# First-block borders by half rows, gain as a row, and turns with one PSUM bank per half of the tokens

## The reference, cut to what matters

```
first block, per layer l:
    h = h + 0.5 * rms_norm(swiglu(rms_norm(h, ffn1_pre_g)), ffn1_post_g)
    u = rms_norm(h, mix_pre_g);  four mixers on u @ w_in, merged by gates
    h = h + rms_norm(merged @ w_o, mix_post_g)
    h = h + 0.5 * rms_norm(swiglu(rms_norm(h, ffn2_pre_g)), ffn2_post_g)
second block, per layer i:
    x = layernorm(ALPHA*x + 0.5*swiglu_2(x), ln_g[i,0], ln_b[i,0])
    x = layernorm(ALPHA*x + hybrid_mixer(x), ln_g[i,1], ln_b[i,1])
    x = layernorm(ALPHA*x + 0.5*swiglu_2(x), ln_g[i,2], ln_b[i,2])
rms_norm(x, g) = x * rsqrt(mean(x*x) + 1e-6) * g
```

## Time and profile before

| | |
|---|---|
| Time before, median of 3 runs | 3259.92 us (3257.59 to 3264.05) |
| Profiled execution, its own time | 3261.25 us |
| Its span, first to last instruction | 3259.6 us |
| TensorE busy | 3045.4 us, 93% of the span |
| VectorE busy | 1881.4 us, 58% |
| ScalarE busy | 1340.2 us, 41% |
| GpSimd busy | 524.2 us, 16% |
| Mean granted TensorE clock | 0.966 |

### The profile page before, as it was taken

How to read it: one execution, slowest core, us unless ns; L and a number is a source line. 1 busy time by engine, 2 the same in 40 slices (tenths; PEclk the granted TensorE clock), 3 DMA queues, 4 the chain that set the end, 5 groups by cost and what they waited for, 6 DMA issues and landing times.

```text
span 3259.6 us, 59469 instructions
## 1 busy us (share of the span) xinstructions
PE 3045.4 (93%) x22178; PEld 2883.8 (88%) x22178; DVE 1881.4 (58%) x3364; ACT 1340.2 (41%) x2214; POOL 524.2 (16%) x791
## 2 busy tenths in 40 slices
PE   8999999999999999998898988999989998899998
PEld 7989998998989999897798878989989897899897
DVE  4556876555555876555455467455555546653555
ACT  4344454434334454433334544434333355443332
POOL 0000000000000000000003555440000055456000
PEclk9999999999999999999998999999999999999999
DMA  5544445454554445455663222254546522123453
GB/s 205 186 161 150 140 146 182 165 185 159 185 180 148 140 146 171 166 190 156 191 215 128 95 78 79 79 181 162 202 146 222 178 96 99 66 79 135 164 196 130
DMA packets 72445, 495.51 MB, mean 152 GB/s; under 512 B 8064, under 2 KB 8240, under 8 KB 20176
## 3 DMA queue, kind: packets, MB, share of 16 engines
q1 hardware_dynamic: 67824, 471.95, 42.2%
q0 software_dynamic: 4048, 18.59, 2.1%
q10 hardware_dynamic: 272, 0.99, 0.1%
HBM read 487.31 MB, written 4.19 MB: 151 GB/s over the span
## 4 chain that ended last, share of the span: by engine, by line
issue 71%; PE 16%; POOL 5%; DVE 4%; DVEq 1%; ACT 1%; POOLq 1%; DMA 1%; ACTq 0%; SPq 0%
PE psum L1153 5%; POOL weights_low L942 4%; PE psum L1065 4%; PE psum L1122 1%; PE psum L1263 1%; POOL small L898 1%; DMA weight_ring<-stream 1%; PE psum L1490 1%; DVE work L2260 1%; POOLq L897 1%; PE psum L1367 1%; PE psum L1209 1%; PE psum L1488 0%; PE psum L1478 0%; ACT weights_high L1558 0%
## 5 line engine op out<-in xcount | busy, mean ns | idle before, releaser
L1558 ACT ACTIVATE weights_high<-weight_ring 128x2048 fp32r<-128x2048 f32 (+5 forms) x778 | 906.0, 1184 | 1121.1 <-DMA weight_ring<-stream 1113.9
L1881 DVE TENSOR_TENSOR weights_low<-weight_ring,weights_high 128x2048 fp32r<-128x2048 f32 (+4 forms) x538 | 888.1, 1658 | 789.7 <-ACT weights_high L1558 786.8
L1065 PE MATMUL psum<-normed_t_high,weights_high 128*128 128x256 f32 x2816 | 801.4, 285 | 11.3 <-DVE normed_t_low L1890 9.9
L1065 PE MATMUL psum<-normed_t_low,weights_high 128*128 128x256 f32 x2816 | 798.9, 284 | 0.0
L1065 PE MATMUL psum<-normed_t_high,weights_low 128*128 128x256 f32 x2816 | 798.6, 284 | 0.0
L1065 PEld LDWEIGHTS psum<-normed_t_high,weights_high 128*128 128x128 f32 x2816 | 541.7, 192 | 17.7 <-DVE normed_t_low L1890 12.3
L1065 PEld LDWEIGHTS psum<-normed_t_low,weights_high 128*128 128x128 f32 x2816 | 542.4, 193 | 3.2
L1065 PEld LDWEIGHTS psum<-normed_t_high,weights_low 128*128 128x128 f32 x2816 | 542.1, 193 | 0.0
L1122 PE MATMUL psum<-weights_high,work_parts 128*128 128x512 f32 x1472 | 464.1, 397 | 13.5 <-DVE work_parts L1890 13.5
L942 POOL TENSOR_TENSOR weights_low<-weight_ring,weights_high 128x256 fp32r<-128x256 f32 x560 | 410.6, 765 | 223.3 <-ACT weights_high L1558 223.3
L1153 PE MATMUL psum<-normed_t_high,weights_high 128*128 128x256 f32 x1248 | 392.1, 314 | 2.8 <-DVE normed_t_low L1890 2.1
(11 more groups left out here) (267 smaller groups left out, 4347.0 us busy)
## 6 DMA issues: line engine op xcount, KB each, us to landing
weight_ring<-stream SPq DMA_DIRECT2D x400, 1024.0 KB, 4.9
weight_ring<-stream SPq DMA_DIRECT2D x64, 768.0 KB, 4.2
feature_rows<-feat POOLq DMA_DIRECT2D x6, 1024.0 KB, 7.6
work<-toeplitz_rows POOLq DMA_DIRECT2D x8, 512.0 KB, 6.5
feature_rows<-feat POOLq DMA_DIRECT2D x6, 512.0 KB, 4.1
toeplitz_rows<-work POOLq DMA_DIRECT2D x1, 3072.0 KB, 36.6
params<-prms POOLq DMA_DIRECT2D x5, 251.5 KB, 3.6
residual<-x SPq DMA_DIRECT2D x2, 512.0 KB, 4.8
```

The source lines that it names most:

```text
L1065: ins = pe.matmul(PS[:, bank, at:at + S], w[a][:, first + k, c * P:(c + 1) * P], src[b][:, k, :], start=(k, m) == (0, 0), stop=(k, m) == ( ...
L1558: return act.activation(dst, src, ACT.Copy, scale=scale)
L1881: dve.tensor_tensor(some(LOW, i, q, n), some(RING, i, q, n), some(HIGH, i, q, n).bitcast(F32), ALU.subtract).then_inc(low_by_vector, n)
```

## The change

- **post**: ScalarE sums the squares of each half row as soon as its bank is full (four Squares of 128x512 into a buffer of its own, `SQ`). GpSimd adds the two sums (`rsqrt_of_halves`: add, drain, add, drain, power). VectorE multiplies each bank by the gain row already behind the Square, without the root (`gained`), and then adds root x product to `H` in one instruction per half row, with a drain behind each (`added`).
- **norm**: ScalarE squares each half row. VectorE scales `H` by the root and by the gain row of the norm, `PG[:, 1]`, into `XN`, four instructions of 128x512, in place of the two scaled identities. Both gain rows come with one transfer of 1024 KB. The first one of the kernel has a transfer of its own at the start.
- **xt in both blocks**: a bank now holds one half of the tokens and four feature blocks (jobs in the order t = 0 half 0, t = 0 half 1, t = 1 half 0, t = 1 half 1). TensorE turns `XN` by transposes in both blocks. In the first block ScalarE copies a bank in one 128x512 and VectorE subtracts in one 128x512. In the second block ScalarE needs four 128x128 per bank for gain and bias. The first product waits for the banks of both t before k = 0 and again before k = 4.
- **post2**: `scaled` runs in two instructions of 128x512, each with its own signal.

The diff, cut to its core (left out: the plans' signal counts, credits, the parameter table without its three gains, and the layout on the host):

```diff
+def rsqrt_of_halves(dst, halves, eps, signal, count):
+    for n in range(2):
+        pool.wait_ge(squares_summed, reach("squares_summed", count + n))
+        pool.tensor_tensor(dst, dst if n else EPSES[:, EPS_AT[eps], 0:1], halves[:, n:n + 1], ALU.add)
+        pool.drain()
+    pool.tensor_tensor(dst, dst, HALFNEG[:, 0:1], ALU.pow).then_inc(signal, 1)
...
-    pool.wait_ge(residual_ready, reach("residual_ready", 2 * st.s if now.blk == 1 else 4 * (st.s + 1)))
+    pool.wait_ge(residual_ready, reach("residual_ready", 4 * st.s if now.blk == 1 else 4 * (st.s + 1)))
     if now.blk == 2 and st.s == 1:
         pool.wait_ge(delta_out_ready, reach("delta_out_ready", NH_B))
     if now.blk == 1:
-        row = feat1[bass.ds(now.l, 1), st.s:st.s + 1, :].rearrange("a b n -> (a b) n")
-        pool.dma_start(PG[:, 0, :], row.to_broadcast([P, D])).then_inc(feature_rows_loaded, 16)
-    else:
-        row = feat2[bass.ds(now.l, 1), st.s].rearrange("a c n -> a (c n)")
-        pool.dma_start(PG[:].rearrange("p c n -> p (c n)"), row.to_broadcast([P, 2 * D])
-                       ).then_inc(feature_rows_loaded, 16)
+        normed = named(("norm", st.s)).at["normed_ready"]
+        pool.wait_ge(normed_ready, reach("normed_ready", normed))
+    row = (feat1 if now.blk == 1 else feat2)[bass.ds(now.l, 1), st.s].rearrange("a c n -> a (c n)")
+    pool.dma_start(PG[:].rearrange("p c n -> p (c n)"), row.to_broadcast([P, 2 * D])
+                   ).then_inc(feature_rows_loaded, 16)
...
+pool.dma_start(PG[:, 1, :], feat1[0, 3, 1:2, :].to_broadcast([P, D])).then_inc(feature_rows_loaded, 16)
...
-        if fresh is not None and k % 2 == 0:
-            ready = named(("xt", fresh)).jobs[k // 2]
-            pe.wait_ge(bank_taken[ready.bank], taken_at(ready))
+        if fresh is not None and k % 4 == 0:
+            for t in range(T):
+                ready = named(("xt", fresh)).jobs[2 * t + k // 4]
+                pe.wait_ge(bank_taken[ready.bank], taken_at(ready))
...
-    n = named(("norm", st.s)).at["normed_ready"] if now.blk == 1 else 2 * st.s
-    for t in range(T):
-        pe.wait_ge(normed_ready, reach("normed_ready", n - 1 + t))
-        for k in range(KB):
-            job = st.jobs[k // 2]
-            if t == 0 and k % 2 == 0:
-                pe.wait_ge(bank_taken[job.bank], turn_at(job))
-            dst = PS[:, job.bank, (k % 2 * T + t) * P:(k % 2 * T + t + 1) * P]
-            if now.blk == 1:
-                ins = pe.matmul(dst, H[:, t, k * P:(k + 1) * P], DG[:, t, :], start=True, stop=True, skip_group_check=True)
-            else:
-                ins = pe.transpose(dst, XN[:, t, k * P:(k + 1) * P], IDENT)
-            if t == T - 1 and k % 2:
-                ins.then_inc(bank_full[job.bank], 1)
+    first = (named(("norm", st.s)).at["normed_ready"] if now.blk == 1 else 4 * st.s) - 3
+    for n, job in enumerate(st.jobs):
+        t, half = n // 2, n % 2
+        pe.wait_ge(bank_taken[job.bank], turn_at(job))
+        pe.wait_ge(normed_ready, reach("normed_ready", first + n))
+        for kk in range(4):
+            k = 4 * half + kk
+            ins = pe.transpose(PS[:, job.bank, kk * P:(kk + 1) * P], XN[:, t, k * P:(k + 1) * P], IDENT)
+        ins.then_inc(bank_full[job.bank], 1)
...
 def norm(st):
-    for t in range(T):
-        act.wait_ge(residual_ready, reach("residual_ready", 2 * st.s - 1 + t))
-        act.activation(XN[:, t, :], H[:, t, :], ACT.Square, scale=D ** -0.5,
-                       accum_out=SS[:, t:t + 1]).then_inc(squares_summed, 1)
+    for n in range(2 * T):
+        t, cols = n // 2, slice(n % 2 * HALF, (n % 2 + 1) * HALF)
+        act.wait_ge(residual_ready, reach("residual_ready", 4 * st.s - 3 + n))
+        act.activation(XN[:, t, cols], H[:, t, cols], ACT.Square, scale=D ** -0.5,
+                       accum_out=SSN[:, n:n + 1]).then_inc(squares_summed, 1)
...
-    for k2, job in enumerate(st.jobs):
+    for n, job in enumerate(st.jobs):
+        t, half = n // 2, n % 2
         act.wait_ge(bank_full[job.bank], full_at(job))
-        b = job.bank
+        src = PS[:, job.bank, :].rearrange("p (k n) -> p k n", k=4)
         if now.blk == 1:
-            g = prm(f"g{st.s}", 1)
-            for kk in range(2):
-                k = 2 * k2 + kk
-                last = copy(XTH[:, k, :], PS[:, b, kk * S:(kk + 1) * S], g[:, k:k + 1])
-            last.then_inc(activation_high_ready, 1)
+            copy(turned(XTH, t, half), src).then_inc(activation_high_ready, 1)
         else:
-            if k2 >= 2:
-                before = st.jobs[k2 - 2]
+            if n >= 2:
+                before = st.jobs[n - 2]
                 act.wait_ge(bank_taken[before.bank], taken_at(before))
-            for kk in range(2):
-                k = 8 * st.s + 2 * k2 + kk
-                last = act.activation(XTF[:, k2 % 2, kk * S:(kk + 1) * S], PS[:, b, kk * S:(kk + 1) * S],
-                                      ACT.Identity, scale=prm("ing", 2)[:, k:k + 1],
-                                      bias=prm("inb", 2)[:, k:k + 1])
+            for kk in range(4):
+                k = 8 * st.s + 4 * half + kk
+                last = act.activation(XTF[:, n % 2, kk * P:(kk + 1) * P], src[:, kk, :], ACT.Identity,
+                                      scale=prm("ing", 2)[:, k:k + 1], bias=prm("inb", 2)[:, k:k + 1])
             last.then_inc(activation_high_ready, 1)
...
 def post(st):
-    for t in range(T):
-        j0, j1 = st.acc.jobs[2 * t], st.acc.jobs[2 * t + 1]
-        act.wait_ge(bank_full[j0.bank], full_at(j0))
-        act.wait_ge(bank_full[j1.bank], full_at(j1))
-        act.activation(XN[:, t, :], PS[:, j0.bank:j0.bank + 2, :].rearrange("p a b -> p (a b)"),
-                       ACT.Square, scale=st.root, accum_out=SS[:, 2 + t:3 + t]
-                          ).then_inc(squares_summed, 1)
+    for n, job in enumerate(st.acc.jobs):
+        if n == 2:
+            act.drain()
+        act.wait_ge(bank_full[job.bank], full_at(job))
+        act.activation(SQ[:, n % 2, :], PS[:, job.bank, :], ACT.Square, scale=st.root,
+                       accum_out=SSP[:, n:n + 1]).then_inc(squares_summed, 1)
...
 def norm(st):
+    dve.wait_ge(feature_rows_loaded, reach("feature_rows_loaded", 16 * st.s))
     for t in range(T):
         dve.wait_ge(rsqrt_ready, reach("rsqrt_ready", st.at["rsqrt_ready"] - 1 + t))
-        dve.tensor_scalar(DG[:, t, :], IDENT, RS[:, t:t + 1], None, ALU.mult).then_inc(normed_ready, 1)
+        for n in range(2):
+            cols = slice(n * HALF, (n + 1) * HALF)
+            dve.scalar_tensor_tensor(out=XN[:, t, cols], in0=H[:, t, cols], scalar=RS[:, t:t + 1],
+                                     in1=PG[:, 1, cols], op0=ALU.mult, op1=ALU.mult
+                                     ).then_inc(normed_ready, 1)
...
-    for k2, job in enumerate(st.jobs):
-        b = job.bank
-
+    for n, job in enumerate(st.jobs):
+        t, half = n // 2, n % 2
+        high, low = (turned(v, t, half) for v in XT)
         if now.blk == 2:
             dve.drain()
         dve.wait_ge(activation_high_ready,
-                    reach("activation_high_ready", st.at["activation_high_ready"] - 3 + k2))
+                    reach("activation_high_ready", st.at["activation_high_ready"] - 3 + n))
         if now.blk == 1:
-            g = prm(f"g{st.s}", 1)
-            for kk in range(2):
-                k = 2 * k2 + kk
-                last = dve.scalar_tensor_tensor(out=XTL[:, k, :], in0=PS[:, b, kk * S:(kk + 1) * S],
-                                                scalar=g[:, k:k + 1], in1=XTH[:, k, :].bitcast(F32),
-                                                op0=ALU.mult, op1=ALU.subtract)
+            whole = PS[:, job.bank, :].rearrange("p (k n) -> p k n", k=4)
+            last = dve.tensor_tensor(low, whole, high.bitcast(F32), ALU.subtract)
         else:
-            high, low = (v[:, 2 * k2:2 * k2 + 2, :].rearrange("p a b -> p (a b)") for v in XT)
-            last = split_here(high, low, XTF[:, k2 % 2, :], False)
-        last.then_inc(bank_taken[b], 1)
+            whole = XTF[:, n % 2, :].rearrange("p (k n) -> p k n", k=4)
+            last = split_here(high, low, whole, False)
+        last.then_inc(bank_taken[job.bank], 1)
...
-    for t in range(T):
+    def gained(t, n):
+        job, cols = st.acc.jobs[2 * t + n], slice(n * HALF, (n + 1) * HALF)
+        dve.wait_ge(squares_summed, reach("squares_summed", st.at["squares_summed"] - 3 + 2 * t + n))
+        dve.tensor_tensor(XN[:, t, cols], PS[:, job.bank, :], PG[:, 0, cols], ALU.mult)
+    def added(t):
+        dve.drain()
         dve.wait_ge(rsqrt_ready, reach("rsqrt_ready", st.at["rsqrt_ready"] - 1 + t))
         for n in range(2):
-            b = st.acc.jobs[2 * t + n].bank
             cols = slice(n * HALF, (n + 1) * HALF)
-            dve.scalar_tensor_tensor(out=XN[:, t, cols], in0=PS[:, b, :], scalar=RS[:, 2 + t:3 + t],
-                                     in1=PG[:, 0, cols], op0=ALU.mult, op1=ALU.mult
```

(19 more changed lines are left out.)

48 lines of the change are left out of this document (27 added, 21 removed).

## The result

The changed kernel takes 3280.11 us (median of 4 runs, 3278.42 to 3284.59) where the kernel before takes 3259.43 (4 runs): a ratio of 1.006, 95% interval 1.0048 to 1.0072, slower by 20.7 us. The forecast was slower by 9.4 us, 3269, with a range that ended at 3279. The direction was right; the forecast size was less than half of what was measured, and the time lies 1 us outside the range. The profiled execution took 3278.42 us, its span is 3276.7.

The account below looks back on a forecast made before the run. TensorE is busy 93% of the span, so borders where it waits decide. Terms -8.4 + 3.2 + 3.2 + 5.1 + 5.2 + 2.2 - 1.5 + 0.4 = +9.4 us on 3261.25 gave 3270.7, stated as 3269; range 3252 to 3279.

Parts of the forecast that it names:

- In-layer borders of the first block: Four borders within first-block layers: product 2.0 us earlier, -2.1 each with later banks, -8.4 in all; clock +3.2.
- The start: Kernel start: first root at 15.4 as before, third low part at 26.1; +3.5 us, clock +1.6.
- The extra 512 KB ... I take nothing: Kernel start: the gain row's transfer may add up to 1.5 us, but should land by the first root; counted as nothing.
- Clock: Behind first products: 4 us at half clock at 0.4 per us, 1.6 per border; 0.8 within first-block layers.
- clock kept by the transposes: Rival, all borders: transposes bring back or keep the clock before the product, taking away 14.4 us: 3255; chance 0.13.
- transposes bring no clock back: Rival, first block's four in-layer borders: they pay the clock in full, +3.2 us: 3272; chance 0.10.
- the rule that I named beside the second rival: TensorE's turns: transposes in that mode are said not to count as busy for the clock; by it 3272.
- GpSimd held: First-block roots: GpSimd waits under VectorE instructions with two SBUF inputs; the rival without this hold: 3265, chance 0.12.
- Between layers: Two weight splits stand ahead of low parts: +1.6 us at 770, +0.6 at 2397, clock +1.6 at each.
- Second block in layers: Four borders within second-block layers: product at 1753.4 instead of 1751.91, half clock no longer hidden; +1.3 us each, +5.2.
- The hand-over's gain: Hand-over to the second block: VectorE has the residual 1.5 us earlier, turns are absorbed; -1.5 us.

Follow-up runs that it names:

- joined kernel: Changed kernel with the second block's turns as before, no transfer on GpSimd's queue at the start, second unit's split behind the evictions at a layer's first product: 3257.13 us.
- spare transposes: Joined kernel plus identity transposes that compute nothing used, put on TensorE at every border: 3271.49 us; with them in the first block alone: 3248.03 us.
- first four runs: Changed kernel with first gain row by SyncE, 3277.85 us; parameters by ScalarE too, 3273.31; one split ahead of the evictions, 3272.98; second block as before, 3271.80.

## Why the prediction was half right

- **In-layer borders of the first block: right.** The product came 10.1 to 10.2 us behind the last matmul's end (forecast 10.8), 9.0 us earlier over the four against 8.4. With what follows it, -4.5 against -5.2.
- **The start: the term that failed, in "The extra 512 KB ... I take nothing".** I bounded it at 1.5 us, by the order on the queue and the row being there in time. The row was there in time. What was late was GpSimd's root, whose drain waited for the parameters behind the row, 5.0 us. With it the term is +9.7 instead of +5.1, and the whole misses the range: without those 5.0 us it would lie inside. The trace of before had the sign of it (its own first root came late, at 15.42, with the squares long summed), and I took that time as given in both kernels without asking what set it. The two runs that took transfers off GpSimd's queue show the cause.
- **Clock: the right mechanism and the right price, too few microseconds.** A microsecond at half clock was priced at 0.4, and it cost that: 1.7 us for 4.0 at 569, 2.0 for 5.1 at 770, 2.2 for 5.3 at the start. Joined with and without spare transposes, the six borders from product to 480th matmul have 13.7 against 45.3 us at half clock and take 384.3 against 398.5: 0.45 each. Mis-sized was how long it stays: I took 4 us between layers (1.6), it was 5.1 at 770, 5.3 at the start and 6.0 at 2397; within a layer I took 0.8, and it was 1.7 at 569 and 1324. At 217 and 974 no half clock stood directly behind the product, but at 974 3.4 us more of it came later in the stretch and cost 1.4. Over the four the loss was 4.5 against 3.2.
- **Rival "clock kept by the transposes" fell, and so did "transposes bring no clock back".** Half clock stood behind ten of twelve first products, so the clock wasn't kept. But at 217 TensorE did nothing but 16 transposes from where the clock fell to where it rose, 3.4 us into the turns and 1.0 ahead of the product, and in the joined kernel with spare ones it stayed full through a border in which TensorE did only transposes. That stands against the rule that I named beside the second rival (the Trainium skill, TensorE: Matmul & The Clock Gate, Part 4), in these kernels and with this form of transpose; the measurement decides.
- **GpSimd held: right.** At 217 the add is up to 1.78 us long and the powers 0.83 to 1.11 under VectorE instructions with two SBUF inputs, the changed scalings and `added` among them, 0.19 and 0.56 otherwise.
- **Between layers: right in kind.** Splits ahead of the low parts set both, as the run with one split shows. At 770 the product is 2.3 later, where the low part at 781.2 meant 1.8. At 2397 it is 3.0 later, where the one at 2408.6 meant 2.6 (the +0.6 of the sum is what is left after 2.0 won back behind the product). The banks came at the forecast pace, the third low part 4.0 us behind the first cast's start, and the 2.0 were won back. What was over is 0.4 for the product and the clock: 6.0 us at half clock behind it instead of 4, 2.7 us instead of 1.6.
- **Second block in layers: half.** The products came 0.5 to 1.4 us later, forecast 1.5; at 1745 the second half's scaled rows began 6.8 us behind the last matmul, where I had left them at 7.6 as before. In all +2.4 against +5.2. The run with the old second block puts its whole share, 2397 included, at 8.3 us.
- **The hand-over's gain didn't come:** the turns did start 1.7 us earlier (7.6 us behind the last matmul instead of 9.3), but the product was 0.9 later, behind the two splits and the third bank, which the forecast had left out here; the run with one split brings it 1.5 earlier, the one with the second block's old turns 2.7. That what happens there is absorbed was right, and the -1.5 in the sum did not fit that.

By terms, measured minus forecast: start +4.6, 770 +1.1, 2397 +1.4, hand-over +1.1, in-layer borders +0.7 and -2.8, elsewhere +1.6; together 7.7, and 17.1 against 9.4. The last 3.6 us up to the medians' 20.7 are that the profiled execution of before lies 1.8 above its median and that of after 1.7 below; the forecast had counted on 1.3 of the first.

Open: why two in-layer borders (217 and 974) have a full clock behind the product in the changed kernel and lose it in the joined one, and at 217 in three of the first four runs too, with the same instructions; the runs show that it differs, not what decides. It was not tried to put the second block's spare work where it delays nothing at 2397.

## What to carry to other kernels

When a transfer is added to the queue of an engine that also computes, ask for each drain behind it how long that transfer takes to land, even if nobody needs its data. Where a border gets shorter, look at what the clock does behind it: half of the microseconds that the products of the first block's inner borders won (4.5 of 9.0) were lost at half clock, and a few idle transposes that are in nobody's way gave 9 us back. A low clock costs only where TensorE would otherwise have work: behind the second block's old turns about 3 us of it cost nothing. Compare a change with the kernel before after mending both alike: of the 23 us between the changed and the joined kernel 8 were the second block's part of the change taken back, and the rest came from two small mends (transfers off GpSimd's queue, one split ahead instead of two); with these two on both sides, what was left of the change moved the time by nothing measurable.

## What the runs showed of the hardware

GpSimd's drain waited for the landing of the transfers that GpSimd itself had issued: 8.48 us with 512 and 239.5 KB under way, 3.67 with 239.5 KB alone, none with neither. And transposes of a 128x128 fp32 identity, 25 beside the 16 turns of a first-block border within a layer, kept TensorE's granted clock at 1.00 where it had been at 0.50 without them. In TensorE-bound products a microsecond at half clock cost 0.40 to 0.45 us.
